# Modulation rows of four blocks summed on VectorE in a later feed-forward, and norm sums with the squares as moving operand

## The reference, cut to what matters

```python
for layer in range(2):                                   # first block
    mod_x = silu(c)     @ mod_w[layer] + mod_b[layer]    # 1024 x 6144
    mod_c = silu(c_ctx) @ mod_w[layer] + mod_b[layer]
    shm, scm, gm, shf, scf, gf = split(mod, 6)           # for x and for ctx
    x = layer_norm(ALPHA * x + gm * mixer(x * (1 + scm) + shm), ...)
    x = layer_norm(ALPHA * x + gf * swiglu(x * (1 + scf) + shf, ...), ...)
# second block, the same with nine vectors of 1024
mod   = silu(c)     @ w_ada + b_ada                      # 1024 x 9216
mod_c = silu(c_ctx) @ w_ada + b_ada
h = rmsnorm(x, g) * (1 + scale) + shift
x = x + w * gate * rmsnorm(y, g)
# rmsnorm: x * rsqrt(mean(x * x) + eps) * g
```

## Time and profile before

| | |
|---|---|
| median of three runs | 3950.0 us (3945.5 to 3950.17) |
| the profiled execution | 3940.22 us, span of its instructions 3938.3 us |
| TensorE busy with matmuls | 3730.9 us, 95% |
| VectorE, ScalarE, GpSimd busy | 49%, 39%, 34% |
| granted TensorE clock, mean | 0.984 |
| DMA | 342.99 MB, 28.4% of the 16 engines' time |

### The profile page before, as it was taken

One profiled execution on the slowest core, in us unless ns is written; L12 is line 12 of the kernel. 1 busy time (PEld: TensorE's weight loads), 2 busy tenths in 40 slices (PEclk: granted clock), 3 DMA queues, 4 the chain that ended last, 5 costly groups with the idle time before them and its releaser, 6 DMA issues.

```text
span 3938.3 us, 52901 instructions
## 1 busy us (share of the span) xinstructions
PE 3730.9 (95%) x21907; PEld 3152.6 (80%) x21907; DVE 1944.4 (49%) x2968; ACT 1543.3 (39%) x2460; POOL 1330.9 (34%) x837
## 2 busy tenths in 40 slices
PE   7999989999999999998999999999989989999999
PEld 5877667889987677676888889999877777788887
DVE  4455566444356666766212354445458745432123
ACT  4133445333235433424422453333355527443223
POOL 2010003334343424426232434434434424353224
PEclk9999999999999999999999999999999999999999
DMA  5221123333332121124333432222422211242333
GB/s 185 74 84 33 44 91 127 99 102 107 97 115 88 33 63 50 38 59 139 106 103 102 134 107 67 68 67 71 153 74 65 59 39 41 70 143 83 98 97 108
DMA packets 463226, 342.99 MB, mean 87 GB/s; under 512 B 18073, under 2 KB 433803, under 8 KB 462987
## 3 DMA queue, kind: packets, MB, share of 16 engines
q1 hardware_dynamic: 462304, 339.35, 28.4%
q10 hardware_dynamic: 683, 0.26, 0.0%
HBM read 334.32 MB, written 5.24 MB: 86 GB/s over the span
## 4 chain that ended last, share of the span: by engine, by line
PE 77%; DVE 9%; ACT 5%; POOL 3%; DMA 3%; issue 2%; SPq 0%; ACTq 0%; POOLq 0%; DVEq 0%
PE PS L107 76%; DVE A L124 2%; PE PS L115 2%; ACT A L118 1%; POOL RWr L124 1%; POOL TM L124 1%; DVE A L132 1%; ACT L118 1%; ACT RWH L121 1%; DMA MW<-in_w_ada 1%; DMA MW<-in_mod_w 1%; DVE RWr L124 1%; DVE SM L144 1%; DVE TM L132 1%; DVE XT L124 1%
## 5 line engine op out<-in xcount | busy, mean ns | idle before, releaser
L124 POOL TENSOR_TENSOR RWr<-RW,RWH 128x1024 fp32r<-128x1024 f32 (+2 forms) x304 | 685.1, 2256 | 1590.7 <-ACT RWH L121 1584.6
L107 PE MATMUL PS<-HTH,RWH 128*128 128x512 f32 (+2 forms) x2688 | 989.2, 368 | 26.7 <-DVE HTr L124 8.6
L107 PE MATMUL PS<-HTr,RWH 128*128 128x512 f32 (+2 forms) x2688 | 956.4, 356 | 0.0
L107 PE MATMUL PS<-Ar,RWH 128*128 128x256 f32 (+2 forms) x3584 | 906.6, 343 | 20.2 <-DVE Ar L124 7.5
L107 PE MATMUL PS<-HTH,RWr 128*128 128x512 f32 (+3 forms) x2528 | 903.0, 357 | 0.0
L107 PEld LDWEIGHTS PS<-Ar,RWH 128*128 128x128 f32 x3584 | 622.8, 191 | 114.2 <-issue 21.8
L107 PE MATMUL PS<-Ar,RWr 128*128 128x256 f32 (+2 forms) x1792 | 607.3, 339 | 0.0
L107 PEld LDWEIGHTS PS<-HTH,RWH 128*128 128x128 f32 x2688 | 511.9, 190 | 118.1 <-issue 34.9
L121 ACT ACTIVATE RWH<-RW 128x1024 fp32r<-128x1024 f32 (+2 forms) x478 | 474.1, 999 | 319.2 <-DMA RW<-in_ffn_w_out 135.1
L107 PEld LDWEIGHTS PS<-HTr,RWH 128*128 128x128 f32 x2688 | 512.5, 191 | 64.1 <-issue 6.5
L107 PEld LDWEIGHTS PS<-HTH,RWr 128*128 128x128 f32 (+1 forms) x2528 | 481.3, 190 | 64.1 <-issue 0.2
(11 more groups left out here) (211 smaller groups left out, 4782.4 us busy)
## 6 DMA issues: line engine op xcount, KB each, us to landing
RW<-in_ffn_w_in SPq DMA_DIRECT2D x176, 512.0 KB, 3.8
MW<-in_mod_w SPq DMA_DIRECT2D x83, 512.0 KB, 4.0
MW<-in_w_ada SPq DMA_DIRECT2D x72, 512.0 KB, 4.4
RW<-in_ffn_w_out SPq DMA_DIRECT2D x80, 384.0 KB, 3.5
RW<-in_ffn_w_out SPq DMA_DIRECT2D x52, 512.0 KB, 3.8
RW<-in_mix_w_in SPq DMA_DIRECT2D x41, 512.0 KB, 3.8
RW<-in_ssd_w_in SPq DMA_DIRECT2D x40, 512.0 KB, 3.9
RW<-in_ev_w_in SPq DMA_DIRECT2D x24, 512.0 KB, 3.9
```

Source lines behind the costliest of these rows:

```text
L107: return self._ins(self.real and self.real.matmul(o, l, r, start=start, stop=stop, skip_group_check=True))
L124: return self._ins(self.real and self.real.tensor_tensor(out=o, in0=i0, in1=i1, op=op))
```

## The change

Three things are changed.

1. Of the modulation, only 10 rows (62 to 71) are left in f0. All later places (transition to ssd, ssd, transition to f1) keep their number of rows and do rows that are 24 lower. The 24 rows that are now left over, and the 8 that f1 had, are rows 96 to 127 (blocks 12 to 15, `FOLD`), and stand in f1, one by one after its steps 2 to 45.
2. These 32 rows are not multiplied on TensorE. VectorE multiplies the whole 128 x 1024 row by silu(c) of each partition (one scalar per partition) and adds it to an accumulator in SBUF, and the same for silu(c_ctx): two instructions per row. At the end of a block TensorE sums the two accumulators over the partitions, with columns of ones and zeros (`sel`) as weights (step `sum`: eight matmuls of 256 columns), into the place where the rows' result stood.
3. The sums of squares of the norms take a 128 x 32 piece of `mean` (1/1024 everywhere) as weights and the squares as moving operand: per 128 tokens one matmul of 128 columns into its own 32 partitions. The root and the reciprocal then work on 128 (or 64) partitions x 128 elements, and `spread` picks the rows with a column of the identity.

The context loads and the first norm of `b1`, which stand in f1, move to later steps of f1 (elements 72 to 108 of the list, before 24 to 80), and the additions of `late` reach to 28 (before 18). The tables of the empty matmuls follow the new numbers of the rows.

```diff
@@ Rows.fetch
-            y.wait_ge("pe.row", was)
+            y.wait_ge("v.row" if was // 8 in Mod.FOLD else "pe.row", was)
...
@@ Mod
+    FOLD = (12, 13, 14, 15)
...
         while n and self.at < upto:
-            out += self.turn(self.at // 8)
+            b, kk = divmod(self.at, 8)
+            if b - 1 not in self.FOLD:
+                out += self.turn(b)
+            elif kk == 5:
+                out += self.turn(b)
+            elif kk == 2 and self.summed < b - 1:
+                out += self.sums(b - 1)
             out.append((self, "row", self.at))
...
+        elif step == "sum":
+            pv = k.banks.take(p, 1, "mod", i)
+            for x in range(2):
+                p.wait_ge("v.row" if x else "v.macc", 8 * i + 7)
+                for j in range(4):
+                    last = p.mm(pv[32 * j:32 * j + 32, 0:256], k.sel[:, 1 - x:33 - x],
+                                self.acc[i][x][:, 256 * j:256 * j + 256], x == 0, x == 1)
+            last.then_inc("pe.msum", i)
...
+        if step == "row" and i // 8 in self.FOLD:
+            b, kk = divmod(i, 8)
+            raw, cs = k.rows.place(i), k.CS[:, self.todo[b][3], kk, :]
...
+            v.wait_ge(k.rows.event(i), i)
+            for x in range(2):
+                acc = self.acc[b][x]
+                if kk == 0:
+                    made = v.ts(acc, raw, cs[:, x:x + 1], None, ALU.mult)
+                else:
+                    v.wait_ge("v.row" if x else "v.macc", i - 1)
+                    made = v.stt(acc, raw, cs[:, x:x + 1], acc, ALU.mult, ALU.add)
+                made.then_inc("v.row" if x else "v.macc", i)
@@ Spread
         for x in range(n // 128):
-            last = p.mm(k.banks.of("var", *key)[:, x:x + 1], sq.bufs[slot][:, 128 * x:128 * x + 128], k.ones[:, 0:1],
-                        i == 0 and x == 0, i == 4)
+            last = p.mm(k.banks.of("var", *key)[32 * x:32 * x + 32, 0:128], k.mean[:, 0:32],
+                        sq.bufs[slot][:, 128 * x:128 * x + 128], i == 0, i == 4)
...
-        s.act(sq.st[:, 0:m], k.banks.of("var", *key)[:, 0:m], ACT.Sqrt, bias=k.epsc, scale=1.0 / D).then_inc(
+        s.act(k.root[part[3]][0:rows, :], k.banks.of("var", *key)[0:rows, 0:128], ACT.Sqrt, bias=k.epsc[0:rows, :]).then_inc(
...
-        v.rcp(sq.st[:, 0:m], sq.st[:, 0:m]).then_inc("v.rstd", *key)
+        v.rcp(st[0:rows, :], st[0:rows, :]).then_inc("v.rstd", *key)
...
-            last = p.mm(pv[:, 128 * x:128 * x + 128], sq.st[:, x:x + 1].to_broadcast([128, 128]), k.ident, True, True)
+            last = p.mm(pv[:, 128 * x:128 * x + 128], k.ident[0:32 * m, 32 * x:32 * x + 1].to_broadcast([32 * m, 128]),
+                        st[0:32 * m, :], True, True)
@@ plan
-    steps = among(ffn.steps(), [("mod", 96)] * 34)
+    steps = among(ffn.steps(), [("mod", 72)] * 10, 0, 250)
...
-    steps = among(ffn.steps(), [("mod", 128)] * 8)
-    steps = among(steps, run(ln, "late", H0, *range(8)) + run(ln, "late", H1, *range(8)), 2, 18)
+    steps = among(ffn.steps(), [("mod", 128)] * 32, 2, 46)
+    steps = [("mod_end", 96), ("mark", "fold.f1")] + among(
+        steps, run(ln, "late", H0, *range(8)) + run(ln, "late", H1, *range(8)), 2, 28)
```

More of the change, by code:

```diff
@@ L540, in vector @@
             v.ms(k.mean[:, :], 1.0 / D)
+            v.ms(k.sel[:, :], 0.0).then_inc("v.sel", 0)
+            v.wait_ge("v.sel", 0)
+            v.ms(k.sel[:, 1:2], 1.0)
             v.ms(k.epsc, EPS)
@@ L580, in __init__ @@
         self.todo += [(a["w_ada_2"][0], k.M2, c, 1, "b_ada", 0) for c in range(9)]
-        self.at, self.turned = 0, 0
+        self.at, self.turned, self.summed = 0, 0, 0
+        wide = lambda *at: [k.A[:, x:x + 1024] for x in at]
+        self.acc = {b: wide(14336 + 2048 * (b % 2), 15360 + 2048 * (b % 2)) for b in self.FOLD}
         k.rows.src = [w[128 * kk:128 * kk + 128, 1024 * c:1024 * c + 1024] for w, _, c, _, _, _ in self.todo for kk in range(8)]
+    FOLD = (12, 13, 14, 15)
     def some(self, n, upto=168):
@@ L594, in turn, with sums @@
         at, self.turned = self.turned, max(self.turned, upto)
-        return [(self, "turn", b) for b in range(at, self.turned)]
+        out = []
+        for b in range(at, self.turned):
+            if b in self.FOLD and self.summed < b:
+                out += self.sums(b)
+            out.append((self, "turn", b))
+        return out
+    def sums(self, b):
+        self.summed = b
+        return [(self, "sum", b)]
     def until(self, upto):
@@ L622, in scalar @@
         k = self.k
-        if step == "row" and i % 8 == 7:
-            b = i // 8
-            s.wait_ge("pe.row", i)
+        if step == "sum" or step == "row" and i % 8 == 7 and i // 8 not in self.FOLD:
+            b = i if step == "sum" else i // 8
+            s.wait_ge(*(("pe.msum", i) if step == "sum" else ("pe.row", i)))
             if b:
@@ L786, in root_scalar @@
     def root_scalar(s, k, key, part):
-        m, sq = (part[1] - part[0]) // 128, k.sums[part[3]]
+        rows, sq = (part[1] - part[0]) // 4, k.sums[part[3]]
         was = sq.before("root", "pe.rstd", *key)
@@ L797, in root_vector @@
     def root_vector(v, k, key, part):
-        m, sq = (part[1] - part[0]) // 128, k.sums[part[3]]
+        rows, st = (part[1] - part[0]) // 4, k.root[part[3]]
         v.wait_ge("s.root", *key)
-        v.rcp(sq.st[:, 0:m], sq.st[:, 0:m]).then_inc("v.rstd", *key)
+        v.rcp(st[0:rows, :], st[0:rows, :]).then_inc("v.rstd", *key)
     @staticmethod
     def root_tensor(p, k, key, part):
-        m, sq = (part[1] - part[0]) // 128, k.sums[part[3]]
+        m, st = (part[1] - part[0]) // 128, k.root[part[3]]
         pv = k.banks.take(p, 1, "rstd", *key)
@@ L4027, in plan @@
              for g in range(4)]
[L4028 to L4029 removed]
+    order += among(ssd.steps([x.steps() for x in mixes[0:3]], [("mod", 88)]), run(ln, "late", X, *range(8)), 4, 30)
+    order += [("mod_end", 88), (scale, "l2", k.M1, 10, (32,))]
     ln = LayerNorm(k, "f1", 1, 0, HX, ALPHA, k.M1, 3, added("m1", 3), ln)
     ffn = Ffn(k, "f1", a["ffn_w_in"][1], a["ffn_w_out"][1], HX, Residual(k, "f1", k.M1, 5, 11, late_of_halves(k, "f1")))
[L4032 removed]
+    order += [(ln, "gain")] + ln_then_head(mixes[3].tail(HX), ln, ffn_head(ffn, HX), pads(8, 96))
     tokens, pre = Tokens(k), Pre(k, "b1", 0, (C, H0, H1), entered)
[L4034 to L4035 removed]
+    steps = among(ffn.steps(), [("mod", 128)] * 32, 2, 46)
+    steps = [("mod_end", 96), ("mark", "fold.f1")] + among(
+        steps, run(ln, "late", H0, *range(8)) + run(ln, "late", H1, *range(8)), 2, 28)
     order += among(steps, [("mark", "ctx2.load")] + tokens.steps() + [(pre, "gain", 1)] + run(pre, "sq", C, 0, 1, 2, 3) +
                    run(pre, "var", C, 0) + run(pre, "sq", C, 4, 5, 6, 7) + root(pre, C, 1) + spread(pre, C) +
[L4038 removed]
+                   run(pre, "norm", C, *range(8)), 72, 108) + [("mod_end", 128)]
     YA = k.A[:, 12288:18432].rearrange("p (m t) -> p m t", t=NT)
@@ L4239, in program @@
         k.ones = sb("ones", [128, 1])
+        k.sel = sb("sel", [128, 33])
         k.mean = sb("mean", [128, 128])
+        k.root = [sb(f"root{i}", [128, 128]) for i in range(2)]
         k.cols = sb("cols", [128, 8])
```

15 lines of the change are left out of this document (11 added, 4 removed).

## The result

The changed kernel takes 3913.0 us (median of 4 runs) against 3947.8 for the kernel before: -34.8 us, a ratio of 0.9905 with a 95% interval of 0.9887 to 0.9924. The forecast was 3926.5, in a range of 3908 to 3950. The two profiled executions differ by less, 3940.2 against 3914.7, -25.5 us, since that of before lay 7.5 us under its median and that of after 1.7 over.

A forecast was written before the change was run, and what follows sets the result against it. TensorE, busy 95% of the span, was taken as close to the only bound in both feed-forwards. The terms -18 - 0.5 + 2 - 10 + 3 = -23.5 us gave a median of 3926.5 us, range 3908 to 3950.

The forecast's parts named there:

- Rows in f0: First feed-forward: 24 rows fewer at 0.67 us each, and a 2.0 us wait saved; -18 us, bounds -13.7 and -18.1.
- the switch: On TensorE, wherever matmuls with 128 columns of weights change to four of 32 beside each other: 0.1 us.
- The wait for `rowb`: End of f0: the transpose waited 2.0 us for ScalarE's copy of the last row; forecast to go, -2.0 us.
- Rows in f1, TensorE: Second feed-forward: eight rows leave TensorE, -5.4 us, and four sums come, +4.9 us; -0.5 us, bounds -1 and +0.
- Rows in f1, VectorE: Second feed-forward: 64 instructions at 1.24 us, 79 us, at most 98; no cost on the path if weights stay in time.
- The queues: SyncE in f1: panel fetches start 3 to 5 us later against 8 us spare; +2 us, bounds 0 and +32.
- the first rival: SyncE's queue in f1: late fetches make each row stall TensorE, deciding from 0.75 us a row; 3966 at 1.25; chance 0.12.
- The sums of squares: In 21 norms, five steps each, at 0.33 us a step plus some 55 visits' 0.1 us: -16 us, 60% counted, -10.
- the root: In 21 norms: reciprocal of 128 elements 0.79 us longer, on the path only where spare time is short; +3 us, bounds 0 and 17.
- The estimate from the Trainium skill: Norms: one column moving has the latency of 60; new form dearer by 28 us, whole change at +15; no chance given.
- The sum: Whole kernel: -18 - 0.5 + 2 - 10 + 3 = -23.5 us, 3916.7 us profiled, 3926.5 us as median.

The follow-up runs named there:

- rows_only: The changed kernel with the four methods of the norms as they were in the kernel before; 3919.1 us, ratio 0.9932 to the kernel before.
- norms_only: The kernel before with the new methods of the norms alone, all 168 rows on TensorE where they were; 3930.9 us, ratio 0.9955 to the kernel before.

## Why the prediction was right

**Rows in f0: -18, right in place, a little small.** The error is the 0.67 us of a row. It took the start of the next matmul as the end of the row's cost, but the switch is paid a second time there. The record behind the row is marked by it, and its distance to the next start is 0.28 where 0.17 is usual:

```profile
1107.57 0.45 PE L107 MATMUL PS<-HTH,RWH 128*128 128x384 f32 x1
1107.85 0.34 PE L107 MATMUL PS<-HTr,RWH 128*128 128x384 f32 x1
```

So a row costs 0.57 + 0.1 + 0.11 = 0.78. 24 of them are -18.7, with the wait of the earlier trace rows -20.7; rows_only shows -20.3 from 600 to 1202 us. The wait for `rowb` is gone, as forecast.

**Rows in f1, TensorE: -0.5.** Eight rows at 0.78 are -6.2, four sums of 1.00 + 0.22 are +4.9: -1.4. Measured from 1877 to 2171 against the earlier trace rows: -1.0.

**Rows in f1, VectorE: free, and so it was, but the term was mis-sized.** 64 instructions took 102.8 us and not 79; the bound of 98 was too low too. The price of 1.24 was nearly right for an instruction that nothing disturbs: 1.28, and 0.75 for the eight with one tensor (seven of them), 78 us for the 64. What the prediction had no term for is GpSimd, which stretched 15 of the accumulations and one of the eight. The means of the rows that it chose between hide the same thing: of the 64 instructions of the earlier trace rows 60 take 1.02 us and four 3.04, each of the four started during an instruction of GpSimd.

**The queues: +2, measured 0.5.** No wait on `RWr` in f1. The prediction called this the tightest cover and it is: with twice the time on VectorE (6 us a row) a row costs 0.8 us, about the rate (0.75) from which it let the first rival decide. But it watched the wrong load. Panels have four buffers; the tokens' load has none, and it is what is late first.

**The sums of squares: -10, and the root +3; measured -17.8 together (12.6 to 22.5).** The price of 0.33 a step was too high: the first costs 0.34, each further one in a visit 0.22. The switch in front was counted for 55 visits (56 in the trace) and the one behind, 33 times before a wide matmul, was not. Coming out of a visit into a wide matmul costs 0.12 in the narrow step (0.34 for a single one and not 0.22) and 0.12 in the matmul behind it. With all of it: 105 x 0.22 + 56 x 0.1 + 33 x 0.24 = 37 us against 56 for the old form (85 x 0.45 + 20 x 0.89), a raw saving of 19 and not 16. The waits for the reciprocals took back 7.6 us in norms_only (9.4 against 1.8), where 3 were forecast, and those for GpSimd's squares 2.3. That ends at -10, and so do the two spans, 3938.3 and 3928.6; but between these two executions the clock went up too (0.984 and 0.986), and by its account that is 7 of the 10. Over the runs it is the same: the mean spans of the group are 3945.0 and 3927.8, 17 us apart, of which the account of the clock has 14.9. What is left for the instructions is 2 us if the clock is charged in full and 7.5 if it is charged at 0.65. So the -7 of the prediction is not refuted, at the upper end of what is left, and the larger part of the measured gain is a thing that the prediction has no term for. Counting records and counting clock overlap, since a matmul at half speed is also a longer one. The estimate from the Trainium skill ("TensorEngine Tiling (Array Packing)", Instruction Overhead) would have made the norms dearer by 28 us before the root; the run shows them cheaper, so the measured 0.11 us a record was the better guide.

**The sum.** By spans -25.5 against -23.5 forecast, and at nearly the same clock (0.984 and 0.983), so this is what the instructions and waits gave. By the medians -34.8. Most of the 9 us between the two is clock: the profiled execution of before had 0.984 where its runs have 0.982, and 0.002 of 3940 us are 8 us, while the runs of the changed kernel have 0.9845. The prediction gave no term to the clock, and that its median still lay 13 us from the measured one and inside the range owes something to luck: the range was wide enough for it. Luck too is how near -23.5 came to -25.5, for the rows gave 21 us or more where 16.5 were counted, and the norms at equal clock 2 to 7.5, where 7 were counted.

## What to carry to other kernels

Price a matmul that is moved out of a stream of another shape from the last start before it to the second start behind it: here 0.1 us was paid in front of it and 0.11 to 0.12 behind it. Work given to an idle engine is free as long as no load queued behind it lacks a buffer; look for the load with the fewest buffers ahead of it, not for the most frequent. And do not take a duration from the mean of a group before you have seen whether it is one duration: here 1.74 us stood for 1.28 and up to 3.45, and the difference was what GpSimd was doing at the time. When two kernels differ by less than 1%, write the mean clock of their runs beside the times: for the norms alone it accounts for 7 of the 10 us between the spans, and by the same account for 15 of the 17 between the means of the runs.

## What the runs showed that was not expected

The mean granted clock differs by form of work in the transitions, not only by chance: 0.9819 over the runs of before and 0.9856 over those of norms_only in the same group, 15 us of time. Some 30 us fewer at the lower level of the clock (1.2 GHz), out of about 140, would make that up. The widest difference between the profiled executions is in the transition into the second mixer, the same times of both (the work in them is not quite the same, since norms_only gains on the other there), norms_only first and the kernel before second:

```profile
2760.00:2990.00 230.00, 206.01 (x1325) 171.19 (x1324) 135.96 (x216) 110.19 (x160) 96.64 (x66) 0.96 0.35 108
```

```profile
2760.00:2990.00 230.00, 211.75 (x1277) 181.51 (x1277) 128.62 (x210) 106.31 (x154) 92.87 (x63) 0.93 0.34 105
```

TensorE issued more instructions (1325 against 1277) in less busy time there. From the same weight panel to the same weight panel, 2795.8 to 3022.3 us before and 2797.3 to 3016.6 in norms_only, it took 7.2 us less, most of what the two spans differ by.
